# Memory attention on split operands, with the next head's query halves between scores and values

## The reference, cut to what matters

```python
hq, hm = rmsnorm(x, g_mem_q), rmsnorm(mem, g_mem_kv)
q = (hq @ w_mem_q).reshape(B, S, 4, 256)
k = (hm @ w_mem_k).reshape(B, M, 4, 256)
v = (hm @ w_mem_v).reshape(B, M, 4, 256)
s = einsum('bshd,bmhd->bhsm', q, k) * 256 ** -0.5
p = softmax(s, axis=-1)
x = x + einsum('bhsm,bmhd->bshd', p, v).reshape(B, S, 1024) @ w_mem_o
```

## Time and profile before

| | us |
|---|---|
| median of 3 runs | 1810.91 |
| lowest, highest | 1809.84, 1811.93 |
| the profiled execution's own time | 1812.46 |
| its span in the profile | 1810.6 |
| mean granted clock of TensorE, of full | 0.973 |

### The profile page before, as it was taken

One profiled execution on the slowest core, in us unless ns is written; L12 is line 12 of the kernel. 1 busy time (PEld: TensorE's weight loads), 2 busy tenths in 40 slices (PEclk: granted clock), 3 DMA queues, 4 the chain that ended last, 5 costly groups with the idle time before them and its releaser, 6 DMA issues.

```text
span 1810.6 us, 23333 instructions
## 1 busy us (share of the span) xinstructions
PE 1717.8 (95%) x8416; PEld 1419.5 (78%) x8416; DVE 1230.3 (68%) x1641; ACT 708.4 (39%) x1326; POOL 861.1 (48%) x659
## 2 busy tenths in 40 slices
PE   7998899999999999889999898999999999999997
PEld 6886788877788888779767687877888888877886
DVE  6754578776877776436344533777888788789965
ACT  5114577776233313124111201443444443543444
POOL 3343344443522340410212233458988888679851
PEclk9997899999999999989999999999999999999999
DMA  5230010110111113114100122125533544695342
GB/s 189 82 117 13 24 36 24 36 48 1 52 43 47 36 58 129 47 30 155 60 23 24 34 82 93 35 82 198 191 125 120 175 144 146 203 332 180 117 134 93
DMA packets 78595, 170.07 MB, mean 94 GB/s; under 512 B 7644, under 2 KB 24220, under 8 KB 78368
## 3 DMA queue, kind: packets, MB, share of 16 engines
q1 hardware_dynamic: 67944, 135.71, 23.2%
q10 hardware_dynamic: 10552, 33.05, 4.8%
HBM read 133.06 MB, written 35.67 MB: 93 GB/s over the span
## 4 chain that ended last, share of the span: by engine, by line
PE 57%; DVE 17%; POOL 10%; ACT 7%; issue 7%; DMA 1%; ACTq 0%; SPq 0%; DVEq 0%; POOLq 0%
PE ps L994 13%; PE ps L997 13%; PE ps L998 13%; DVE x_t L2530 4%; PE ps L1173 3%; ACT x_t L1832 2%; POOL sum_s L905 2%; PE ps L1250 2%; PE ps L1144 2%; POOL w_lo L899 2%; PE ps L1334 2%; DVE x_t L2559 2%; PE ps L1192 2%; PE ps L1145 1%; PE ps L1313 1%
## 5 line engine op out<-in xcount | busy, mean ns | idle before, releaser
L994 PE MATMUL ps<-h_hi,w_hi 128*128 128x512 f32 x1108 | 441.1, 398 | 22.7 <-DVE h_lo L2005 7.2
L997 PE MATMUL ps<-h_lo,w_hi 128*128 128x512 f32 x1108 | 436.1, 394 | 0.0
L998 PE MATMUL ps<-h_hi,w_lo 128*128 128x512 f32 x1108 | 435.9, 393 | 0.0
L848 POOL TENSOR_TENSOR w_hi<-w_raw,ones 128x1024 fp32r<-128x1024 f32 x55 | 114.9, 2089 | 613.6 <-PE ps L994 512.8
L994 PEld LDWEIGHTS ps<-h_hi,w_hi 128*128 128x128 f32 x1108 | 210.9, 190 | 76.0 <-issue 9.2
L998 PEld LDWEIGHTS ps<-h_hi,w_lo 128*128 128x128 f32 x1108 | 210.8, 190 | 45.0
L997 PEld LDWEIGHTS ps<-h_lo,w_hi 128*128 128x128 f32 x1108 | 210.9, 190 | 43.4 <-issue 0.7
L876 POOL TENSOR_SCALAR probs<-probs,nsa_inv,gate_sig 128x640 f32<-128x640 f32 (+7 forms) x128 | 100.8, 787 | 176.2 <-DVE nsa_inv L2209 176.0
L2530 DVE SCALAR_TENSOR_TENSOR x_t<-ps,par,x_t 128x1023 f32<-128x1023 f32 x84 | 107.7, 1282 | 80.3 <-ACT x_t L1832 78.8
L851 POOL TENSOR_TENSOR w_lo<-w_raw,w_hi 128x1024 fp32r<-128x1024 f32 x55 | 146.5, 2664 | 4.3
L2005 DVE TENSOR_TENSOR pt_lo<-ps,pt_hi 128x512 fp32r<-128x512 f32 (+1 forms) x148 | 101.8, 688 | 58.9 <-ACT pt_hi L1623 57.1
(11 more groups left out here) (360 smaller groups left out, 4083.0 us busy)
## 6 DMA issues: line engine op xcount, KB each, us to landing
w_raw<-in_w_tiles SPq DMA_DIRECT2D x109, 512.0 KB, 3.5
w_raw<-in_w_tiles SPq DMA_DIRECT2D x55, 256.0 KB, 3.0
s_new<-in_w_tiles SPq DMA_DIRECT2D x44, 256.0 KB, 4.3
z_dram<-x_t ACTq DMA_DIRECT2D x21, 512.0 KB, 2.9
b<-z_dram SPq DMA_DIRECT2D x33, 256.0 KB, 3.6
q_st<-q_dram SPq DMA_DIRECT2D x64, 128.0 KB, 2.9
t_dram<-t_new ACTq DMA_DIRECT2D x22, 256.0 KB, 5.1
s_dram<-s_new SPq DMA_DIRECT2D x22, 256.0 KB, 3.0
```

What stands on the lines that cost most here:

```text
L848: pool.tensor_tensor(w_hi[s][:, :], w_raw[s][:, :], ones[:, :].to_broadcast([P, KT * P]), ALU.mult).then_inc(w_hi_made.sem, w_hi_made.up())
L994: ins = mm(out_ap, whi, x_hi, start=first, stop=False)
L997: mm(out_ap, whi, x_lo, start=False, stop=False)
L998: return mm(out_ap, wlo, x_hi, start=False, stop=last)
```

## The change

- **Split operands.** xk, xv, xq and xp_t each become a high and a low part. Where VectorE copied a block out of ps, ScalarE now writes the high part and VectorE the low part behind it (it waits for `hi_ready`). A score block is six products of 256 columns, a value block six of 512, both through fp32r parts.
- **Heads written out.** The loop over heads is gone. MEM_ORDER is one list for all heads. The first head's four query blocks stand ahead; in heads 0 to 2 the next head's query blocks stand behind s3, s7, v1 and v3; the last head has the old order. xv_h is gone.
- **The norm.** `spread_roots` before the values, its copy to r_bc and the parts of col are gone. ScalarE's exponential takes `scale=col[:, i]`, and VectorE multiplies the negated maximum by the same column first. The queries are scaled by 1/16 only.
- **Banks.** The ring has 8 banks from the turning of the values to the end of the attention, and TensorE no longer waits for all of them before the queries. The key tiles' high parts are made by ScalarE in its loop over weight tiles, and VectorE splits the next weight tile before it takes a key block.
- **Space.** The new low parts lie over tiles 2 to 7 of x_t (and xp_t_lo over the places of acc and r_bc). ScalarE stores these six tiles (3072 KB) to x_dram before the keys and loads them back behind the splits of xo; VectorE waits for the load before the residual adds, and both engines wait for the store before they write there.

```diff
+MEM_BODY = (("s", 0), ("s", 1), ("s", 2), ("s", 3), ("q", 0), ("t", 0), ("s", 4), ("s", 5), ("t", 2), ("s", 6), ("s", 7),
+            ("q", 1), ("t", 4), ("v", 0), ("t", 6), ("v", 1), ("q", 2), ("v", 2), ("v", 3), ("q", 3))
...
 # TensorE
-            gemm_loop(KT // 4, 4, hm_hi, hm_lo, MEM)
-            spread_roots()
-            gemm_loop(KT // 4, 4, hm_hi, hm_lo, MEM)
+            gemm_loop(KT // 2, 4, hm_hi, hm_lo, MEM)
             freed_now()
+            ring.resize(8)
...
+            def x_scores(h, i):
+
+                if i == 0 or i == 4:
+                    taken(made_q[h, 2 if i == 0 else 3])
+                b, q = open_chunk(), slice(i * P, i * P + P)
+                for z in range(2):
+                    k = 2 * h + z
+                    mm(ps[:, b, 0:MEM], xq_hi[:, z, q], xk_hi[:, k, :], start=z == 0, stop=False)
+                    mm(ps[:, b, 0:MEM], xq_hi[:, z, q], xk_lo[:, k, :], start=False, stop=False)
+                    last = mm(ps[:, b, 0:MEM], xq_lo[:, z, q], xk_hi[:, k, :], start=False, stop=z == 1)
...
+                for j in range(MEMT):
+                    last = product(ps[:, b, :], (xv_hi[:, j, vs], xv_lo[:, j, vs]), xp_t_hi[:, j, cs], xp_t_lo[:, j, cs],
+                                   j == 0, j == MEMT - 1)
...
 # ScalarE
+            x_parked = t("x_parked", 16)
+            act.dma_start(x_dram[PARK:KT, :, :].rearrange("k p s -> p k s"), x_t[:, PARK:KT, :]).then_inc(
+                x_parked.sem, x_parked.up())
...
+                    act.wait_ge(x_shift_ready.sem, x_shift_ready.next())
+                    f(xp[i % 4][:, :], ps[:, b, 0:MEM], ACT.Exp, bias=shift[:, i % 4:i % 4 + 1], scale=col[:, i:i + 1],
+                      accum_out=sums[:, i % 4:i % 4 + 1]).then_inc(x_exp_ready.sem, x_exp_ready.up())
...
             split_hi(xo, 0, 2 * KT)
+            act.dma_start(x_t[:, PARK:KT, :], x_dram[PARK:KT, :, :].rearrange("k p s -> p k s")).then_inc(
+                xh_loaded.sem, xh_loaded.up())
...
 # VectorE
+                    ts(shift[:, i % 4:i % 4 + 1], shift[:, i % 4:i % 4 + 1], col[:, i:i + 1], None, ALU.mult).then_inc(
+                        x_shift_ready.sem, x_shift_ready.up())
...
             clear_sums(acc)
+            dve.wait_ge(t("xh_loaded", 16).sem, t("xh_loaded", 16).next())
             residual_loop()
```

More of the change, by code:

```diff
@@ L1298, in _ @@
             pe.wait_ge(h_ready.sem, h_ready.value())
-            freed_now()
[L1300 to L1329, removed]
-                    pe.wait_ge(chunk_freed.sem, chunk_done.value(chunk_done.n - made_t[4 * c + 2]))
-                    b = open_chunk()
-                    for j in range(MEMT):
-                        last = mm(ps[:, b, :], xv_h[:, j, z * P:z * P + P], xp_t[:, j, c * HALF:c * HALF + HALF],
-                                  start=j == 0, stop=j == MEMT - 1)
-                    last.then_inc(chunk_done.sem, chunk_done.up())
[L1338 to L1343, removed]
-                        if i == 0:
-                            pe.wait_ge(xv_ready.sem, xv_ready.next())
-                        x_values(i)
@@ new lines, in _, with taken, x_queries @@
+            made_q, made_s, made_t, query_slot = {}, {}, {}, [0]
+            def taken(made):
+                pe.wait_ge(chunk_freed.sem, chunk_done.value(chunk_done.n - made))
+            def x_queries(h, n):
+                if n % 2 == 0:
+                    query_slot[0] = next_weights()
+                s, cs = query_slot[0], slice(n % 2 * HALF, n % 2 * HALF + HALF)
+                b = open_chunk()
+                for k in range(KT):
+                    w = (w_hi[s][:, k * P:k * P + P], w_lo[s][:, k * P:k * P + P])
+                    last = product(ps[:, b, :], w, h_hi[:, k, cs], h_lo[:, k, cs], k == 0, k == KT - 1,
+                                   tag=(n % 2 == 0 and k == 0))
+                last.then_inc(chunk_done.sem, chunk_done.up())
+                made_q[h, n] = chunk_done.n
@@ L1347, in _ @@
+            for what, h, i in MEM_ORDER:
+                if what == "q":
+                    x_queries(h, i)
+                elif what == "s":
+                    x_scores(h, i)
+                elif what == "t":
+                    x_turn(h, i)
+                else:
+                    x_values(h, i)
+            freed_now()
+            ring.resize(4)
             gemm_tile(h_hi, h_lo, wait_piece=each_piece)
@@ new lines, in _ @@
+            ring.resize(8)
+            for j in range(MEMT):
+                for q in range(2):
+                    b = chunk()
+                    f(xv_hi[:, j, q * HALF:q * HALF + HALF], ps[:, b, :], ACT.Copy).then_inc(hi_ready.sem, hi_ready.up())
+            act.wait_ge(x_parked.sem, x_parked.value())
+            for what, h, i in MEM_ORDER:
+                if what == "q":
+                    b = chunk()
+                    z, cs = i // 2, slice(i % 2 * HALF, i % 2 * HALF + HALF)
+                    f(xq_hi[:, z, cs], ps[:, b, :], ACT.Copy, scale=XDH ** -0.5).then_inc(hi_ready.sem, hi_ready.up())
+                elif what == "s":
@@ new lines, in _ @@
+                    waiting.append(i)
+                    if len(waiting) > 1:
+                        finish()
+                    continue
+                while waiting:
+                    finish()
+                b = chunk()
+                if what == "q":
+                    z, cs = i // 2, slice(i % 2 * HALF, i % 2 * HALF + HALF)
+                    wait_hi()
+                    ins = low(xq_lo[:, z, cs], ps[:, b, :], xq_hi[:, z, cs], XDH ** -0.5)
+                elif what == "t":
+                    wait_hi()
+                    hi = xp_t_hi[:, :, i * P:i * P + 2 * P]
+                    ins = low(xp_t_lo[:, :, i * P:i * P + 2 * P], ps[:, b, :].rearrange("p (j q) -> p j q", j=MEMT), hi)
+                else:
+                    ins = dve.tensor_copy(xo[:, 2 * h + i % 2, i // 2 * HALF:i // 2 * HALF + HALF], ps[:, b, :])
```

151 lines of the change are left out of this document (84 added, 67 removed).

## The result

The changed kernel takes 1787.49 us (median of 4 runs, 1785.20 to 1792.96), the kernel before, run beside it, 1810.38 (4 runs, 1809.53 to 1811.93). The ratio is 0.9874, with an interval of 0.9859 to 0.9889: 22.9 us less, between 20.1 and 25.5.

What follows compares the result with a forecast made beforehand. The prediction took the stage as bound by TensorE's order of work, with gaps. Its terms, 14.4 - 0.7 + 1.6 + 1.6 = 16.9 us, taken from 1810.91, gave 1794.0 us, range 1788.5 to 1800.

Steps and rivals of the forecast that it cites:

- Part 2: Heads 0 to 2, next head's query halves between scores and values: no TensorE waits, 34.8 us a head, 14.4 us less in all.
- Part 1: Attention's score and value products on split operands: 1.16 and 1.42 us less, together 2.6 us of TensorE's work a head.
- Part 3: Last head, without query halves as cover: 18.4 us (bounds 15.1 and 20.5), 0.7 worse than before.
- Part 4: Between keys and values, the norm as the exponential's scale replaces 16 spreading products: 1.6 us less (bounds 0 and 1.74).
- Part 5: Start of the queries, TensorE no longer waits for the value copies: 1.6 us less (bounds 0 and 1.66).
- Part 6: Storing six eighths of x before the keys and reading it back after the attention: costs nothing, 9 us of cover.
- Removing the loop makes no term: Query stage: all products run at the same distance with or without the loop, so nothing was counted.
- the clock's rival: One slow-clock stretch of TensorE more (1797.3) or less (1790.7), 3.3 us each; chance 0.08 together.
- the prediction's own low case: Last head at 15.1 us with one slow-clock stretch less: 1787.4 us.
- GpSimd's block of the row scaling: Rival in the heads: GpSimd's weight splitting delays VectorE's row scaling, up to 4.3 us in a chain; 1800.3 us, chance 0.12.
- The chain did not bound the heads: Rival: the VectorE-ScalarE chain bounds every head, the order hides nothing, only 3.2 us remain; 1807.7 us, chance 0.04.
- the read-back did not come late: Rival: x landing after about 1060 stops TensorE at the third output tile; slower than the old kernel from 1077; chance 0.03.

## Why the prediction was right and wrong

- **What bounds it, and Part 2, the order**: right. 34.81 us a head against 34.8, with TensorE busy throughout (the working has turn 4 open at 17.6 where its terms add to 17.5, which changes nothing); the waits that were expected to vanish vanished, and came back when the query halves moved behind the head.
- **Part 1, split operands**: right in kind and size, 2.58 us a head against 2.6 by the run with plain products. That the longer chain must be hidden was Part 3's reasoning, and the run without the interleaving shows it for every head: 0.66 us more in place of a gain, though the norm's multiplication is in that chain too.
- **Part 3, the last head**: right, 18.70 against 18.4 on TensorE's landmarks; on the same landmarks the old last head took 18.11, so +0.6 against +0.7.
- **Part 4, the spread**: the term that was mis-sized. I took 1.6 with an upper bound of 1.74, the time of the 16 products; the stretch gave 3.2, of which the run with the spreading put back returns 2.8: 1.72 for the products, as priced, and 1.09 for a weight load that took 4.4 us beside a transfer of instructions. The bound counted the removed products and nothing else that goes with them. The earlier trace rows could not show it: they are from the one profile of six in which no load was that late, and in the other five one copy stands 3.7 to 4.1 us behind the copy before it. The changed kernel's copies run at an even 2.93 us:

```profile
830.51 1.06 ACT L1784 ACTIVATE w_hi<-w_raw 128x1024 fp32r<-128x1024 f32 x1 [1.59 <-DMA w_raw<-in_w_tiles]
...
833.45 1.06 ACT L1784 ACTIVATE w_hi<-w_raw 128x1024 fp32r<-128x1024 f32 x1 [1.60 <-PE ps L1012]
```

- **Part 5, start of the queries**: 1.90 against 1.6. Queries follow the transposes by 1.72 us; before it was 3.62, from the first row here to the product at 870.75 in the earlier trace rows.

```profile
867.13 1.97 PE L1035 MATMUL ps<-ident,xv_feat 128*128 128x128 f32 x16 [0.52 <-DVE xv_feat L2427]
```

The wait of 1.66 is counted from the modelled end of the transposes, 1.97 us behind their start, while in a dense stream the next product starts 1.72 behind it. So a bound taken from a wait alone was 0.24 too low.

- **Part 6, parking x**: right. The store landed 9.1 us after its issue, the read-back 11.2. The read-back was issued at 1006.81, 3 us behind the last output copy and before ScalarE was through with its splits, so earlier than I had it. The weight load beside it took 6.6 us in place of some 3.2, and no wait of TensorE followed. VectorE's first output add waits 0.87 us for TensorE and not for the load, and stands 17.14 us behind that copy, where the earlier trace rows have 19.73. These are the page's part 6 and VectorE's timeline:

```profile
x_dram<-x_t ACTq DMA_DIRECT2D x1, 3072.0 KB, 9.1
x_t<-x_dram ACTq DMA_DIRECT2D x1, 3072.0 KB, 11.2
```
```profile
1020.99 1.23 DVE L2431 TENSOR_TENSOR x_t<-ps,x_t 128x1024 f32 x1 [0.87 <-PE ps L1016]
```

- **"Removing the loop makes no term"**: the statement holds for the sum and not for the loop. Written out alone it gives 1.7, 1.3 and 2.0 us in the stage by its three profiles, and 6.3 and 4.7 timed. What it gives in the stage are shorter waits, 0.22 a head and 0.34 ahead of the queries, and Parts 2 and 5 had already counted these waits as gone whole. Its timed gain beyond the stage is the open remainder.
- **The sum**: 16.9 forecast, 18.9 in the stage. Of the 2 us, 1.6 are Part 4 and 0.4 Parts 3 and 5. With these alone the time would have been 1792.0, well inside the range.
- **Everything outside the stage, priced at nothing**: the step that failed. The sum held the code ahead of the stage and behind it to be the same in time because it is the same in text, and left any difference to the clock's rival, with 0.08. The timed gain has 4.0 us more than the stage (1.2 to 6.6 by the interval), the profiles 1.6. The profiles show what moves there: the stretches of lower clock, and with them the way up to the stage, by 5 to 7 us between executions of one kernel; whether the change itself moves them, and so where the 4 us come from, stays open. The range was too narrow besides: its lower end, 1788.5, lay above the prediction's own low case, 1787.4. That the measured 1787.49 is near that case is luck, since the last head took 18.7 and not 15.1.
- **Rivals.** GpSimd's block of the row scaling is real, as the timing said: the mean rose from 353 to 573 ns, and beside GpSimd's two instructions it took 1.26 and 1.79 us, ending 0.15 us behind each of them.

```profile
918.89 1.89 POOL L866 TENSOR_TENSOR w_hi<-w_raw,ones 128x1024 fp32r<-128x1024 f32 x1 [12.11 <-PE ps L1012]
920.86 2.40 POOL L869 TENSOR_TENSOR w_lo<-w_raw,w_hi 128x1024 fp32r<-128x1024 f32 x1
```
```profile
919.67 1.26 DVE L2523 TENSOR_SCALAR xp<-xp,sums 128x256 f32<-128x256 f32 x1
...
921.62 1.79 DVE L2523 TENSOR_SCALAR xp<-xp,sums 128x256 f32<-128x256 f32 x1
```

A head loses 0.9 + 1.4 = 2.3 us of VectorE's time to it, not 4.3, and the cover of two microseconds or more swallowed it: no wait of TensorE followed. This is the lock that the Trainium skill describes in "SBUF — State Buffer", section "Who interferes with whom"; by the two rows the trace agrees. The 1.4 us a head that this rival was priced at does not follow from the delays that it names, 0.6 and 2.3 us. The chain did not bound the heads, and the read-back did not come late. The clock's rival gave one stretch more or less a chance of 0.08. Its size, 3.3 us a stretch, was a little high for the one stretch that can be compared, 2.5 us (44.9 against 42.4). Single executions of one kernel differ by more than one such stretch, which the three timed runs of before that the prediction had, 2.1 us apart, did not tell.

## What to carry to other kernels

When a small step leaves a stage, the time of its own products is no upper bound: here a weight load behind it landed 1.1 us late as well, and only further profiles of the old kernel show that. Splitting operands shortens TensorE's work (2.6 us a head here) and lengthens the chain from one product to the next, so look for independent products to put between them; without them this change lost 0.66 us a head. Before giving a range, ask how far executions of the unchanged kernel lie apart: its stage was the same to 1.3 us, the way up to it only to 5.

## What the runs showed of the hardware

The exponential with its scale read from a column took 565 ns in the mean, against 472 with the bias alone in the kernel before: 93 ns for each of 32, on ScalarE and off the path, where Part 4 had taken it as free. The Trainium skill, "ScalarE: Activation LUTs", section "What ACT_TABLE_LOAD costs", has 93 ns for each operand that is a pointer to a column, and the trace agrees. The maximum's multiplication by the norm on a 128x1 column took 214 ns on VectorE. Written out, the exponentials need one load of ScalarE's function tables of 1.28 us, in the loop they had four. A weight load of 512 KB landed 4.0 to 4.7 us after its issue beside one transfer of instructions (0.02 MB) in nine of ten profiles, and in 3.0 to 3.7 us at other times in the last part of the key and value stage.
